# The compression of keys and values on four column tiles of 32, summed and turned by one matmul with an adding table

## What is computed

```python
def compress(kv, w1, w2, pe):
    B, T, G, Dh = kv.shape                                  # 1, 256, 2, 64
    nc = (T - CMP_BLOCK) // CMP_STRIDE + 1                  # (256 - 32) // 16 + 1 = 15
    idx = jnp.arange(nc)[:, None] * CMP_STRIDE + jnp.arange(CMP_BLOCK)[None, :]
    blocks = kv[:, idx] + pe[None, None, :, None, :]
    blocks = jnp.swapaxes(blocks, 2, 3).reshape(B, nc, G, CMP_BLOCK * Dh)
    return jax.nn.gelu(blocks @ w1) @ w2                    # 2048 -> 128 -> 64
```

## Time and profile before

| what | value |
|---|---|
| median of 3 runs | 1940.83 us (1940.30 to 1942.86) |
| profiled execution, first to last instruction | 1941.0 us |
| TensorE busy | 1832.4 us, 94% of the span, 12118 records |
| VectorE busy | 746.2 us, 38% |
| ScalarE busy | 615.3 us, 32% |
| DMA | 592.8 MB, mean 305 GB/s |
| granted TensorE clock, mean | 0.984 |

### The profile page before, as it was taken

How to read it: one execution, slowest core, us unless ns; L and a number is a source line. 1 busy time by engine, 2 the same in 40 slices (tenths; PEclk the granted TensorE clock), 3 DMA queues, 4 the chain that set the end, 5 groups by cost and what they waited for, 6 DMA issues and landing times.

```text
span 1941.0 us, 29827 instructions
## 1 busy us (share of the span) xinstructions
PE 1832.4 (94%) x12118; PEld 1257.7 (65%) x12118; DVE 746.2 (38%) x1575; ACT 615.3 (32%) x1093; POOL 85.7 (4%) x104
## 2 busy tenths in 40 slices
PE   5999999999999999998999999999999999999997
PEld 3855899999899999967444445444444444444446
DVE  2575677556677645275122121121121121221216
ACT  3466555444455445375111111111111111110115
POOL 0010111000111001001000000000000000000001
PEclk8999999999999999989899999999999999999998
DMA  9638555554555545105999999999999999999991
GB/s 395 245 159 342 219 185 183 185 228 174 191 207 189 177 177 184 68 1 197 372 424 426 423 428 424 425 427 426 425 428 425 426 427 426 426 427 425 428 423 47
DMA packets 64941, 592.80 MB, mean 305 GB/s; under 512 B 6000, under 2 KB 9328, under 8 KB 10448
## 3 DMA queue, kind: packets, MB, share of 16 engines
q1 hardware_dynamic: 64416, 589.75, 74.6%
q10 hardware_dynamic: 432, 1.71, 0.2%
HBM read 590.39 MB, written 1.05 MB: 305 GB/s over the span
## 4 chain that ended last, share of the span: by engine, by line
PE 52%; DMA 28%; DVE 11%; ACT 6%; issue 3%; SPq 1%; ACTq 0%; POOL 0%; DVEq 0%
DMA ring<-in_experts 27%; PE ps L2364 15%; DVE wd_lo L1175 6%; ACT wd_hi L717 4%; PE ps L2374 3%; PE ps L1857 3%; PE ps L1853 3%; PE ps L1854 3%; PE ps L2351 2%; PE ps L2133 2%; PE ps L2128 2%; PE ps L2129 2%; PE ps L1907 2%; PE ps L1871 1%; PE ps L1872 1%
## 5 line engine op out<-in xcount | busy, mean ns | idle before, releaser
L2364 PE MATMUL ps<-ring,A 128*64 128x512 f32 x2112 | 468.5, 597 | 38.8 <-ACT A L1057 22.8
L2364 PEld LDWEIGHTS ps<-ring,A 128*64 128x64 f32 x2112 | 168.8, 137 | 333.7 <-issue 333.0
L1716 DVE TENSOR_TENSOR A<-ps,W 128x512 f32<-128x512 f32 x66 | 45.4, 688 | 788.8 <-PE ps L2401 788.8
L1175 DVE TENSOR_TENSOR wd_lo<-ring,wd_hi 128x2048 fp32r<-128x2048 f32 x107 | 245.3, 2296 | 185.2 <-ACT wd_hi L717 185.2
L1853 PE MATMUL ps<-aL_hi,wd_hi 128*128 128x256 f32 x1040 | 256.8, 285 | 3.7 <-ACT wd_hi L717 2.0
L1854 PE MATMUL ps<-aL_lo,wd_hi 128*128 128x256 f32 x1040 | 254.9, 283 | 0.0
L717 ACT ACTIVATE wd_hi<-ring 128x2048 fp32r<-128x2048 f32 x107 | 203.8, 1906 | 118.1 <-PE ps L2133 69.8
L2374 PE MATMUL ps<-ring,A 128*64 128x512 f32 x1056 | 233.9, 595 | 0.0
L1853 PEld LDWEIGHTS ps<-aL_hi,wd_hi 128*128 128x128 f32 x1040 | 199.4, 192 | 6.4 <-issue 5.2
L1854 PEld LDWEIGHTS ps<-aL_lo,wd_hi 128*128 128x128 f32 x1040 | 199.5, 192 | 0.1
L1046 ACT ACTIVATE A<-ps 128x512 f32<-128x512 f32 x66 | 39.4, 597 | 472.6 <-PE ps L2364 472.6
(11 more groups left out here) (364 smaller groups left out, 2197.9 us busy)
## 6 DMA issues: line engine op xcount, KB each, us to landing
ring<-in_experts SPq DMA_DIRECT2D x198, 2048.0 KB, 17.2
ring<-in_weights SPq DMA_DIRECT2D x161, 1024.0 KB, 5.0
hT<-in_x SPq DMA_DIRECT2D x1, 1024.0 KB, 7.6
hT<-in_ctx SPq DMA_DIRECT2D x1, 1024.0 KB, 15.0
hT<-in_weights SPq DMA_DIRECT2D x1, 1024.0 KB, 5.7
tab<-in_tables ACTq DMA_DIRECT2D x1, 768.0 KB, 10.4
out<-aT SPq DMA_DIRECT2D x2, 384.0 KB, 2.5
A<-in_tables SPq DMA_DIRECT2D x1, 548.0 KB, 6.0
```

What stands on the lines that cost most here:

```text
L1175: dve.tensor_tensor(wd_lo[:, b], cell(PLAN[name]["first"][k]["cell"]), wd_hi[:, b].bitcast(F32), ALU.subtract).then_inc(split_lo, 1)
L1716: dve.tensor_tensor(m_gl[:, j].rearrange("p c h n -> p (c h) n"), ps[:, 6 + j, :].rearrange("p (c n) -> p c n", c=8), b_up[:, bass.ds(e * ...
L2364: mm = pe.matmul(ps[h * CAP:(h + 1) * CAP, 4 + j, :], xg[:, c, :], w[:, c, h], start=(c == 0), stop=(c == KC - 1))
```

## The change

TensorE's accumulations are spread over four column tiles: term l goes to tile l mod 4, rows 32t and up of the same bank, so that after 32 matmuls four partial sums of 8 terms each lie below one another in 128 rows. The position vectors are now broadcast to 32 columns, so that every row of the 128 is written. ScalarE copies all 128 rows to SBUF without Gelu. One matmul for each k, with the copied rows as weights and a table `add_tiles` (128 x 32, a one where the row number mod 32 is the column) as the moving operand, adds the four parts and turns them. Gelu follows behind this, on ScalarE, from PSUM straight into `hid`; the two copies on VectorE that did this fall away. VectorE makes the table once, by a reduction of the identity, at the head of `block2_in`; a new semaphore `cmp_tiles` lets TensorE wait for it.

```diff
-        hid_rows = A[0:BLOCKS, 10560:10816].rearrange("p (k n) -> p k n", k=2)
+        hid_rows = A[:, 10560:10816].rearrange("p (k n) -> p k n", k=2)
+        add_tiles = A[:, 7760:7792]
...
             def compress2():
                 for k in range(2):
                     act.wait_ge(cmp_proj, k + 1)
-                    act.activation(hid_rows[:, k, :], ps[0:BLOCKS, 4 + k, 0:P], ACT.Gelu_apprx_tanh).then_inc(cmp_act, 1)
+                    act.activation(hid_rows[:, k, :], ps[:, 4 + k, 0:P], ACT.Copy).then_inc(cmp_act, 1)
+                for k in range(2):
+                    act.wait_ge(cmp_turned, k + 1)
+                    act.activation(hid[:, k, 0:BLOCKS], ps[:, 4 + k, T:T + BLOCKS], ACT.Gelu_apprx_tanh).then_inc(cmp_hid, 1)
...
             def block2_in():
-                def step(ins):
-                    ins.then_inc(gate_x, 1)
-
+                dve.tensor_reduce(add_tiles, ident.rearrange("p (t m) -> p m t", t=4), AX_X, ALU.add).then_inc(cmp_tiles, 1)
                 for k in range(2, 5):
                     split_item("w_in", k)
...
                 def hidden():
-                    for k in range(2):
-                        dve.wait_ge(cmp_turned, k + 1)
-                        dve.tensor_copy(hid[:, k, 0:BLOCKS], ps[:, 4 + k, T:T + BLOCKS]).then_inc(cmp_hid, 1)
                     dve.wait_ge(cmp_hid, 2)
...
-                    out, kv = ps[0:BLOCKS, 4 + k, 0:P], kvc[:, k].rearrange("p g t -> p (g t)")
+                    kv = kvc[:, k].rearrange("p g t -> p (g t)")
                     for l in range(16):
-                        pe.matmul(out, pos[:, l:l + 1].broadcast_to([P, BLOCKS]), w[:, l, :], start=(l == 0), stop=False)
+                        t = l % 4
+                        pe.matmul(ps[32 * t:32 * t + 32, 4 + k, 0:P], pos[:, l:l + 1].broadcast_to([P, 32]), w[:, l, :],
+                                  start=(l < 4), stop=False, skip_group_check=True)
                     for l in range(16):
-                        mm = pe.matmul(out, kv[:, 2 * l:2 * l + CMP_STRIDE * (BLOCKS - 1) + 1:CMP_STRIDE], w[:, l, :],
-                                       start=False, stop=(l == 15))
+                        t = l % 4
+                        mm = pe.matmul(ps[32 * t:32 * t + BLOCKS, 4 + k, 0:P], kv[:, 2 * l:2 * l + CMP_STRIDE * (BLOCKS - 1) + 1:CMP_STRIDE],
+                                       w[:, l, :], start=False, stop=(l >= 12), skip_group_check=True)
                     mm.then_inc(cmp_proj, 1)
             def compress2_out():
+                pe.wait_ge(cmp_tiles, 1)
                 for k in range(2):
                     pe.wait_ge(cmp_act, k + 1)
-                    pe.transpose(ps[:, 4 + k, T:T + BLOCKS], hid_rows[:, k, :], ident[0:BLOCKS, 0:BLOCKS]).then_inc(cmp_turned, 1)
+                    pe.matmul(ps[:, 4 + k, T:T + BLOCKS], hid_rows[:, k, :], add_tiles[:, 0:BLOCKS], start=True, stop=True).then_inc(cmp_turned, 1)
```

More of the change, by code:

```diff
@@ L398, in build @@
         cmp_proj, cmp_act, cmp_turned = sem("cmp_proj"), sem("cmp_act"), sem("cmp_turned")
-        cmp_hid, cmp_out, cmp_ready = sem("cmp_hid"), sem("cmp_out"), sem("cmp_ready")
+        cmp_hid, cmp_out, cmp_ready, cmp_tiles = sem("cmp_hid"), sem("cmp_out"), sem("cmp_ready"), sem("cmp_tiles")
         b_s, b_x, b_l, b_slope = (sem(n) for n in ("b_s", "b_x", "b_l", "b_slope"))
```

## The result

The changed kernel takes 1932.57 us in the median of 4 runs (1930.79 to 1933.02), the kernel before 1941.54 beside it (4 runs). The two medians are 9.0 us apart. The ratio of the runs is 0.9949, with a 95% interval of 0.9938 to 0.9961, that is 9.9 us less, between 7.6 and 12.0. The forecast was 1931.2, in a range of 1929.3 to 1934.6.

The account below looks back on a forecast made before the run. TensorE's compression was taken to bound the place ahead of `scores(0)`, by 15.6 us. Gain 9.6 us: 10.5 from TensorE, 0.9 given back on ScalarE; 1941.0 - 9.6 = 1931.4 profiled, median 1931.2, range 1929.3 to 1934.6.

Parts of the forecast that it names:

- 32 steps, 5.07 us: Compression on TensorE: 32 groups of four at 109 ns each, 218 at half clock, 5.07 us; `scores(0)` at 805.3 instead of 815.8.
- ScalarE: Copies, two table loads, Gelus, exponentials and keys decide `cmp_scores`, at 810.8, 1.2 us later than VectorE; 0.9 us given back.
- 0.2 us late for nothing: Compression's end: it may come 0.2 us later without cost, since ScalarE's second copy starts only at 805.5.
- The table: VectorE's reduction making the table, 0.28 us, behind the first split of `w_in` in 2.73 us of idle time: costs nothing.
- Shift to the end: Expert stage: an earlier attention starts the expert weight stream earlier, so its shift passes to the end one for one.
- The sum's base: Starting figure: profiled span 1941.0 us, taken as 0.2 above the median of the kernel before.
- Rival 1: Compression: tiles overlap only in part; at twice the time a group, 3.3 us lost, giving 1934.5; chance 0.13.
- Rival 3: Compression: tiles run one after the other, ScalarE's chain stands behind, 0.7 us later than before: 1941.5; chance 0.03.
- Rival 4: Compression: column tiles' weight loads don't hide, about 229 ns a record, 16 us more, 1957; chance 0.02.
- Rival 5: ScalarE: each table load costs more than its record, at most 0.19 us each, 1931.6 for both; chance 0.02.
- Rival 2: TensorE's clock: one half-clock stretch more 1932.9, one less 1929.5, chance 0.12; none behind the compression 1926, chance 0.03.

Follow-up runs that it names:

- added load: Changed kernel plus a useless one-column Sqrt on ScalarE behind the two copies, bringing one more table load; 1933.83 us, one run.
- the keys' order: Changed kernel with ScalarE copying the compressed keys ahead of unit 0's exponentials; median 1930.63 us, ratio 0.9947 to the kernel before; again 1930.54, 0.9941.
- the copies on VectorE: Changed kernel with VectorE instead of ScalarE copying the 128 rows of partial sums to SBUF; median 1932.98 us, ratio 0.9953 to the kernel before.

## Why the prediction was right

**The compression.** "32 steps, 5.07 us" measured 4.89. A group of four cost what one record cost: 32 records, eight groups, take 0.87 us at full clock, a quarter of 3.50, strided weights included. The factor back to back is 4.0, where the Trainium skill ("TensorE: Matmul & The Clock Gate", section "Measured speedup vs the span model") lists 3.07 for four row tiles and 2.38 for three column tiles. Taking the nearest rows of `ada` over the page was right. It was 0.18 us shorter because the clock was at half for its first 2.6 us (800.09 to 802.72) and not 3.2. That gained nothing, since ScalarE decides.

**ScalarE.** It became what decides, as forecast, by 810.35 - 809.2 = 1.1 us over VectorE (forecast 1.2). The added load and the keys' order showed it. The sum came out 0.45 us too late, at 810.8 instead of 810.35: the copies ended 0.33 us behind the gates' logarithm and not 0.57 (the first starts before the logarithm ends, and they overlap), the two Gelus took 0.28 and not 0.4, and the compression began 0.1 us earlier in this trace. So the compressed scores moved by 10.07 us, not 9.6. The "0.2 us late for nothing" of the compression was too much: 4.94 - 4.89 is 0.05.

**The table.** The reduction for the table took 0.38 us, not 0.28, at 737.42, ahead of an idle time of 6.0 us rather than the one I had pointed to: nothing, as said.

**Shift to the end.** One for one: 10.1 us at the compressed scores, 10.8 at the end of the span; the 0.7 between them is of the size by which the tail differs among traces that do nothing to it (1118.8 to 1120.5).

**The sum's base.** The prediction took the span of before for a time 0.2 us above the median. That reading was wrong: the span stands 1.7 to 2.2 us below its own execution's time, and that execution was the slowest. It did no harm, and that is luck of the arithmetic: 1941.0 - 0.2 is the median of before whatever the span means. The measured 1932.57 is 1.4 us over the forecast. About 0.7 of it is the base, since a fourth run moved the median of before from 1940.83 to 1941.54, and 0.6 is a gain of 9.0 us between the medians instead of 9.6. The traces show 10.8 and the ratio 9.9; with four runs each this difference is within the interval.

**Rivals.** Rival 1 (twice the time a group) did not come: a group took 0.109 us at full clock. Its price was about right: a compression of 9.39 us put the compressed scores 4.4 us later, so one of 8.6 would have cost about 3.6 (estimate), against the 3.3 that it was given. Two tiles at a time was meant as its case and was not, since the overlap stayed. Rival 3 (1941.5) did not come, and even the order with four terms in a row in one tile, made to take the overlap away, gave 1935.99; its 0.7 us for the longer chain is borne out. Rival 4 did not show. Rival 5 did not either: behind both loads on the path the next activation starts within 0.02 us (805.47 + 1.28 to 806.76, 807.06 + 1.28 to 808.36). Rival 2's one stretch more or less is within what the runs spread by; its case of no half clock at all was sized at 5 us, and filling the waits gave 5.2 in medians and, in the traces, 5.0 up to the end of the attention.

## What to carry to other kernels

Where a matmul uses 32 columns of the array and there are several terms to a sum, four column tiles taken in turn can make it a quarter; here they did so for 128 moving columns and strided weights (3.50 to 0.87 us for 32 records). Price the gain on the engine that is next in line, here ScalarE with two table loads that lost their cover. After such a change look at the wait that it leaves on TensorE: filling two waits of 1.3 and 1.9 us with matmuls whose results nobody uses gave 5 us, where the reordering of ScalarE gave 1 us inside the trace, because 17 us at half clock stood behind the waits. The filling did not hold the clock in every run: with fewer fillings single runs took up to 1931.52. And judge changes of one microsecond by intervals inside the trace, since medians of this kernel move by as much with the clock. Compare such intervals at the same length of the stage ahead: the copies on VectorE seemed to bring nothing only because the compression had been 0.4 us longer in that trace.

## What the runs showed of the hardware that I had not expected

- Matmuls in different column tiles leave program order in their starts: a record of a later instruction in tile 0 starts at 803.21, one of an earlier in tile 3 at 803.32. That gave a tile order that should have had no overlap a compression of 9.39 us instead of 15.62.
- With the wait ahead of a sparse piece filled, the clock stayed up through it in all five traces: the compressed scores, 16 columns each, did not bring it down behind a filled wait (1.7 us between first and last record instead of 3.2). Among or behind the gates' 32-column matmuls, which follow dense work, it fell to 0.50 in all traces but one (at 799.30 in the changed kernel's). Why the one and not the other stays open.
- An execution's time lies 1.7 to 2.2 us over its span, in every run here.
